# Three plain column pairs and a down projection ahead of the Strassen pairs, the last pair by token blocks, two weight roundings on ScalarE

## What is computed

```python
h = x * (1 + sc2) + sh2
u = h @ w_up + b_up                      # 1024 -> 5632
uc = conv_b + sum(conv_w[j] * ctx[:, j:j + T] for j in range(3))
a, g = jnp.split(uc, 2, axis=-1)
f = (a * jax.nn.gelu(g)) @ w_down        # 2816 -> 1024
x = layer_norm(ALPHA * x + g2 * f, ln2_w, ln2_b)
```

## Time and profile before

| | us |
|---|---|
| median of 3 runs (1894.36 to 1896.42) | 1895.5 |
| the profiled execution | 1895.79 |
| its span, first to last instruction | 1894.0 |
| TensorE busy in it | 1808.4 (95%) |
| GpSimd busy | 897.0 (47%) |
| VectorE busy | 1115.0 (59%) |
| ScalarE busy | 585.3 (31%) |

### The profile page before, as it was taken

One profiled execution on the slowest core, in us unless ns is written; L12 is line 12 of the kernel. 1 busy time (PEld: TensorE's weight loads), 2 busy tenths in 40 slices (PEclk: granted clock), 3 DMA queues, 4 the chain that ended last, 5 costly groups with the idle time before them and its releaser, 6 DMA issues.

```text
span 1894.0 us, 30856 instructions
## 1 busy us (share of the span) xinstructions
PE 1808.4 (95%) x12279; PEld 1733.2 (92%) x12279; DVE 1115.0 (59%) x2006; ACT 585.3 (31%) x1327; POOL 897.0 (47%) x638
## 2 busy tenths in 40 slices
PE   8999999999999999999999994999999999999884
PEld 6999888888999999899999994999999999999873
DVE  4837875773322324354345857875677567656677
ACT  3213444433222323342111675122122212211235
POOL 0332212212222222133336448688888888888830
PEclk9999999999999999999999996999999999999987
DMA  9443321114333434265333000111111111111102
GB/s 389 166 145 107 122 83 69 57 57 136 98 107 124 124 107 121 84 234 178 125 125 101 12 12 26 44 47 45 46 46 66 46 46 45 68 38 53 46 32 84
DMA packets 78903, 173.42 MB, mean 92 GB/s; under 512 B 9300, under 2 KB 42452, under 8 KB 78632
## 3 DMA queue, kind: packets, MB, share of 16 engines
q1 hardware_dynamic: 55112, 119.63, 18.6%
q10 hardware_dynamic: 23648, 51.82, 7.6%
HBM read 139.19 MB, written 32.24 MB: 91 GB/s over the span
## 4 chain that ended last, share of the span: by engine, by line
PE 84%; DVE 6%; ACT 3%; POOL 2%; DVEq 2%; DMA 1%; issue 1%; ACTq 0%; SPq 0%; POOLq 0%
PE acc L587 38%; PE px L868 12%; PE px L912 7%; PE acc L868 7%; PE acc L912 4%; PE px L834 2%; PE px L658 1%; PE acc L834 1%; PE px L687 1%; PE px L670 1%; PE px L684 1%; PE px L760 1%; PE px L759 1%; PE px L758 1%; PE px L672 1%
## 5 line engine op out<-in xcount | busy, mean ns | idle before, releaser
L587 PE MATMUL acc<-x_hilo_a,w_hilo 128*128 128x352 f32 x4032 | 664.3, 324 | 1.7 <-ACT x_c L1013 1.7
L587 PEld LDWEIGHTS acc<-x_hilo_a,w_hilo 128*128 128x128 f32 x4032 | 643.0, 188 | 9.9 <-issue 9.2
L458 POOL CAST w_hilo<-w_raw 128x1024 fp32r<-128x1024 f32 x71 | 81.3, 1146 | 731.7 <-PE acc L587 623.0
L460 POOL TENSOR_TENSOR w_hilo<-w_raw,w_hilo 128x1024 fp32r<-128x1024 f32 x71 | 184.9, 2604 | 5.7
L494 POOL TENSOR_TENSOR w_unit<-w_raw,w_unit 128x512 fp32r<-128x512 f32 x120 | 177.1, 1476 | 9.6
L868 PE MATMUL px<-x_hilo_a,w_unit 128*128 128x264 f32 x1200 | 157.1, 287 | 2.5 <-DVE x_hilo_a L1873 2.5
L868 PEld LDWEIGHTS px<-x_hilo_a,w_unit 128*128 128x128 f32 x1200 | 152.1, 191 | 2.7 <-DVE x_hilo_a L1873 2.7
L912 PE MATMUL px<-ffn_act,w_unit 128*128 128x352 f32 x900 | 152.5, 325 | 2.1 <-DVE u_row_g L1929 2.1
L912 PEld LDWEIGHTS px<-ffn_act,w_unit 128*128 128x128 f32 x900 | 146.2, 190 | 2.6 <-DVE u_row_g L1929 2.4
L492 POOL CAST w_unit<-w_raw 128x512 fp32r<-128x512 f32 x120 | 122.2, 1019 | 42.3 <-PE px L912 10.8
L1720 DVE SCALAR_TENSOR_TENSOR c_state<-c_state,stage,px 128x257 f32<-128x257 f32 x36 | 17.4, 482 | 207.1 <-PE px L760 207.1
(11 more groups left out here) (322 smaller groups left out, 2929.0 us busy)
## 6 DMA issues: line engine op xcount, KB each, us to landing
w_raw<-in_w_panels SPq DMA_DIRECT2D x141, 512.0 KB, 3.3
z_spill<-stage ACTq DMA_DIRECT2D x41, 528.0 KB, 2.7
adaT_ring<-in_w_adaT SPq DMA_DIRECT2D x32, 512.0 KB, 4.4
stage<-z_spill ACTq DMA_DIRECT2D x20, 528.0 KB, 4.7
ada_ring<-in_w_ada SPq DMA_DIRECT2D x16, 512.0 KB, 13.4
zc<-z_spill SPq DMA_DIRECT2D x8, 1024.0 KB, 9.3
...
```

What stands on the lines that cost most here:

```text
L458: nc.gpsimd.tensor_copy(to[:, 0, :], raw[:, s, :]).then_inc(w_hi, 1)
L460: nc.gpsimd.tensor_tensor(to[:, 1, :], raw[:, s, :], to[:, 0, :].bitcast(F32), ALU.subtract).then_inc(w_ready, 1)
L587: last = mm(acc[:, n, 0:NW], whl[:, slot, wi, k * P:(k + 1) * P], rhs[:, xi, k, n * NW:(n + 1) * NW], start=(k == 0 and j == 0), stop=(k = ...
```

## The change

1. **Three plain pairs.** `SINGLES` lists six plain panels: pair 2 is now plain, and the first Strassen pair is number 3 (`PAIR0`). Its terms stand in another order (A11, S2, A12, S3, S1, A22, S4).
2. **Down 0 ahead of pair 3.** The order is now: six plain panels, down 0, pairs 3 and 4, down 1, and the rest as before.
3. **Preparation moved.** The scaling of `XC` goes from DVE to POOL, four instructions ahead of each of the two added panel splits. ScalarE's and VectorE's lists at the start of the channel half are interleaved anew: the convolution of pair 0 stands between the block sums, `h_full` has two buffers of its own, and T1 is made out of `x_hilo_a` in place during down 0 (`t1_full`, `t1_high`, `t1_low`), since the sixth plain panel still reads the old values.
4. **Last pair by token blocks.** Taps, gelu, product and rounding of pair 21 run in three blocks of 352 (`last_block`, `last_gelu`, `last_round`), and the last down step waits for `fa_lo` block by block.
5. **Two of seven roundings on ScalarE.** The high parts of A12 and A22 are written by ScalarE (`plain_high`, after `first_take`); POOL waits for them and does the low part.

```diff
+SINGLES = ((0, 0), (0, 1), (1, 0), (1, 1), (2, 0), (2, 1))
+NSING = len(SINGLES)
+PAIR0 = 3
-    order = [("u", 0, i) for i in (0, 2, 1, 3)] + [("p", 1, 0), ("d", 0, 0), ("d", 0, 1)]
+    order = [("u", pi, r) for pi, r in SINGLES] + [("d", 0, 0), ("d", 0, 1)]
...
             def round_unit(unit, to, src):
                 count = UNIT_READY[unit]
-                nc.gpsimd.tensor_copy(to[:, 0, :], src).then_inc(w_hi, 1)
-                pool.wait_ge(w_hi, count)
+                if unit[1] in ("A12", "A22"):
+                    pool.wait_ge(a_hi, 2 * (2 * unit[0][1] + unit[0][2] - PAIR0) + (1 if unit[1] == "A12" else 2))
+                    pool.sem_inc(w_hi, 1)
+                else:
+                    nc.gpsimd.tensor_copy(to[:, 0, :], src).then_inc(w_hi, 1)
+                    pool.wait_ge(w_hi, count)
...
+            for kt in range(KH):
+                sums_low(kt)
+            for k in range(KT):
+                nc.gpsimd.tensor_scalar(XC[:, k, :], XC[:, k, :], der[:, 4, k:k + 1], der[:, 5, k:k + 1], ALU.mult, ALU.add)\
+                  .then_inc(xc_rdy, 1)
+                if k % 4 == 3:
+                    split(P_FFN + 4 + k // 4)
...
             def down_ready(j, m, n):
-                if n == 0 and m == 0:
-                    pe.wait_ge(fa_lo, j * 2 + 2)
+                if m == 0 and (n == 0 or j == FF - 1):
+                    pe.wait_ge(fa_lo, j * 2 + (n + 1 if j == FF - 1 else 2))
...
+            def plain_high(pi):
+                item = ("p", pi // 2, pi % 2)
+                for part, s in (("A12", 0), ("A22", 1)):
+                    p = PANEL[item] + s
+                    act.wait_ge(raw_in[p % 2], (p // 2 + 1) * 16)
+                    unit_free(act, (item, part))
+                    A(wu[:, UNIT_SLOT[item, part], 0, :], raw[:, p % 2, HALF:D], ACT.Copy).then_inc(a_hi, 1)
...
+            def t1_full(kt):
+                if kt == 0:
+                    dve.wait_ge(*ready(("u", *SINGLES[NSING - 1], NT - 1)))
+                V.tensor_tensor(u2t[:, :], XA[:, 0, kt, HN:T].bitcast(F32), XA[:, 0, kt, 0:HN].bitcast(F32), ALU.subtract)
+                dve.drain()
+                V.tensor_tensor(u2t[:, :], u2t[:, :], XA[:, 1, kt, HN:T].bitcast(F32), ALU.add)
+                dve.drain()
+                V.tensor_tensor(u2t[:, :], u2t[:, :], XA[:, 1, kt, 0:HN].bitcast(F32), ALU.subtract).then_inc(ts_rdy, 1)
...
+            dve.wait_ge(xc_rdy, KT)
+            down_row(0, 0)
+            t1_full(0)
+            down_row(0, 1)
+            t1_low(0)
+            conv_first(2, 1)
+            down_row(0, 2)
...
-            ffn_conv(2 * FF - 1, 1)
-            ffn_conv(2 * FF - 1, 0)
-            ffn_low(2 * FF - 2)
-            dve.drain()
-            ffn_prod(2 * FF - 1)
-            ffn_low(2 * FF - 1)
+            for n in range(NT):
+                last_block(n)
```

More of the change, by code:

```diff
@@ L264, in build @@
         lsum1 = at("ln_sums", [P, 2, T], o_T)
-        hb = at("h2_full", [P, 2, T], o_T)
-        t1f = after("h2_diff", [P, KH, HN])
+        hb = at("h2_full", [P, 2, 2, T], o_T)
+        assert place["end"] <= o_C
         wo = at("w_out_hilo", [P, KT - 2, 2, D], o_B, F32R)
@@ L272, in build @@
         cs = after("conv_out", [P, FG, 4, 4])
[L273 removed]
+        fc0 = after("ffn_consts_first", [P, 2, 4, 8])
         assert place["end"] <= 229344
@@ L1953, in down_row, with last_block @@
                     down_take(("d", j, m, n))
+            def last_block(n):
+                pi = 2 * FF - 1
+                a, b = n * NW, CW if n == NT - 1 else (n + 1) * NW
+                rows = [ST[:, conv_row(pi, r), a:b] for r in range(2)]
+                for tap in range(2):
+                    for r in (1, 0):
+                        dve.wait_ge(cv_a, row_made(pi, r))
+                        last = V.scalar_tensor_tensor(rows[r], ub[r][:, a + tap:b + tap], consts(pi, r)[:, 1 + tap:2 + tap], rows[r], ALU.mult, ALU.add)
+                        if tap:
+                            last.then_inc(cv_d, 1)
+                    dve.drain()
+                dve.wait_ge(gl_rdy, pi + n + 1)
+                V.tensor_tensor(rows[0], rows[0], rows[1], ALU.mult).then_inc(pr_rdy, 1)
+                for t in range(2):
+                    dve.wait_ge(fa_hi, pi + (n + 1 if t else 0))
+                    for c, d, s in pieces(n):
+                        last = V.tensor_tensor(ft[:, 1, t, c:d], ST[:, conv_row(pi - 1 + t, 0), c + 2 * s:d + 2 * s],
+                                               ft[:, 0, t, c:d].bitcast(F32), ALU.subtract)
+                last.then_inc(fa_lo, 1)
             sums_full(0)
@@ L1962, in _ @@
             t2_low(3)
[L1963 to L1964 removed]
             ffn_conv(1, 0)
[L1966 to L1967 removed]
             ffn_prod(0)
             ffn_conv(1, 1)
[L1970 removed]
             ffn_low(0)
             ffn_prod(1)
[L1973 to L1974 removed]
+            ffn_conv(2, 0)
             ffn_low(1)
[L1976 to L1982 removed]
+            dve.wait_ge(xc_rdy, KT)
[5 more added lines that the diff above has]
+            down_row(0, 2)
+            dve.drain()
+            conv_second(2, 1)
+            t1_full(1)
+            down_row(0, 3)
+            t1_low(1)
+            dve.drain()
+            t1_full(2)
+            down_row(0, 4)
+            t1_low(2)
+            dve.drain()
+            t1_full(3)
+            down_row(0, 5)
+            t1_low(3)
+            ffn_prod(2)
+            down_row(0, 6)
+            down_row(0, 7)
+            for pi in range(PAIR0, 2 * FF):
+                if pi == PAIR0:
+                    u2_take(pi)
+                    u3_take(pi)
+                    c22_take(pi)
+                    ffn_low(2)
+                    c21_take(pi)
+                    c12_take(pi)
+                elif pi % 2 and pi < 2 * FF - 2:
                     j, pv = pi // 2 - 1, pi - 1
```

271 lines of the change are left out of this document (137 added, 134 removed).

## The result

The changed kernel is **slower**: 1907.5 us (median of 4 runs, 1905.1 to 1909.6) against 1895.2 of the kernel before, a ratio of 1.0064 with a 95% interval of 1.0046 to 1.0081. I had forecast 1890.8 and a range up to 1902. The profiled execution took 1907.5 us with a span of 1905.6, 11.6 more than the span before.

What follows compares the result with a forecast made beforehand. TensorE, busy 95% of the span, was taken as the bound, with matmul count and few holes deciding. Start 0, roundings -2.3 and last pair -2.4 gave -4.7: 1890.8 us from 1895.5, forecast band 1886 to 1894, full range 1879.5 to 1902.

Steps and rivals of the forecast that it cites:

- hole: After the fourth plain panel: TensorE waits 26.0 us for POOL's scalings and split of the fifth, where it stood 22.0.
- wait at the start of down 0: Start of down 0: pair 1's product takes some 11.2 us against 11.5 of the sixth panel, a tie.
- down 0: Down 0: VectorE can't keep up, so 6.5 us are lost on top of TensorE's 23.0.
- tail: After pair 21: token blocks let VectorE start taking down tiles earlier, -2.4 us, bounded by -6.4 and +4.4.
- the first rival: Start of the channel half: POOL's scalings run at its two-input rate, together +11.3, giving 1902.1 us; chance 0.16.
- the 1.1 to 1.9 that I had named as a sign of being wrong: Before the fifth panel's split: the forecast would be wrong if one POOL scaling left 1.1 to 1.9 us.
- the -2.3 for the roundings: Pair 21: two casts moved to ScalarE bring POOL's low part 2.3 us earlier, shrinking the hole from 4.92 to 2.6.
- GpSimd would wait for ScalarE in every double pair: Double pairs: a new short hole in each, eight with slow clock costing over 15 us, would prove the forecast wrong.
- The cover that I named: Steady stretch: ScalarE's casts cost zero, since the low parts are due three terms (8.8 us) later.
- The rival that short instructions lose their turns: Last pair: VectorE's short block instructions wait for POOL's, last term +4.4, sum +2.1, 1897.6 us; chance 0.16.
- 34.6 us could be won: Plain work's end to pair 3: if nothing waited, pair 3 would begin at 1186.1, winning 34.6 us; not expected.
- VectorE keeps up: Faster rival in down 0: VectorE keeps up and scalings are cheap, the start gains 9 us, 1882; chance 0.20.

Runs made afterwards that it cites:

- e4: The changed kernel with pair 3's terms in the usual order (S1 third, A12 fifth): 1900.0 us.
- e2: The kernel before with only the high parts of A12 and A22 moved to ScalarE: 1896.3 us, ratio 1.0006.
- e5: The changed kernel with both added panel splits ahead of all eight scalings and pair 3's terms in the usual order: 1891.4 us.
- e6: e5 with all roundings on GpSimd again: 1889.6 us.
- e1: The kernel before with only the last pair by token blocks: 1895.3 us, ratio 0.9995.
- e11: e6 with the last pair whole again instead of by token blocks: 1889.8 us.
- e10: e9 with the roundings back on GpSimd and the first T1 block ahead of pair 1's product: 1887.8 us.
- e7: e5 without two of the three subtractions of each T1 block (output not the reference's): 1885.7 us.
- e9: e5 with panel splits between low-sum blocks, ScalarE's third-row takes before the last full rows, and first tap and gelu before the last high sums: 1888.8 us.
- e12: e10 with the eight scalings on ScalarE instead of GpSimd: 1887.8 us.

## Why the prediction was wrong

Its sum was -4.7, and the spans say +11.6. Step by step:

| step | predicted | measured |
|---|---|---|
| ScalarE's last high sums end | 1150.6 | 1150.7 |
| low sums end | 1154.1 | 1153.9 |
| four scalings | 7.5 | 9.0 |
| split of the fifth panel | 4.4 | 5.3 |
| hole | 26.0 | 29.5 |
| slow clock behind it | 2.4 | 2.2 |
| wait at the start of down 0 | about none (a tie) | none |
| down 0 | 29.5 | 31.2 |
| pair 3 begins | 1221.0 | 1224.5 |
| pair 3 to pair 5 | no change | +7.7 |
| pair 5 to the end of pair 21 | -2.3 | +3.2 |
| tail | -2.4 | -3.2 |

**The start was right in its mechanism and short in three terms.** The order of waits, their releasers and the first two times came as forecast. A scaling alone is 1.21 us (I had 1.15), so the first rival falls. The Trainium skill (GPSIMD Engine Reference, Engine selection) has one-input operations near line rate. The row agrees: 1.21 us where VectorE needs 1.32. What I took too small was the time beside VectorE: 0.7 us on each scaling was 1.04, and 0.6 on the split 1.55. At 2.25 us a scaling lies outside the 1.1 to 1.9 that I had named as a sign of being wrong. In down 0 the loss was 8.2 us instead of 6.5. The holes in it were shorter than forecast, 4.9 us instead of 5.7; the slow clock behind the last was a full one (24 matmuls in 6.94 us, granted clock 0.54 of full from 1217.7 to 1224.5), where I had counted less than half. Pair 3 begins 3.9 us later than before, and as this execution was 1.3 us ahead, the stretch is +5.1 instead of 0. By e4's trace, which has the same instructions there, it is +1.9 (90.4 us), so of the 5.1 up to 3.2 are the scatter of single executions.

**The step that failed is a term put at nothing without a reason: pair 3 to pair 5.** The changed order of pair 3's terms stood in my own description of the change, and in no term of the sum (0 - 2.3 - 2.4). It costs 7.5 us (e4), the largest single item of the miss. In the sum itself the step that failed is the -2.3 for the roundings, where that stretch came out at +3.2 and the roundings alone at +2.4 (e2) to +3.2 (e5 to e6). A slot of a ring is handed on in the order of the terms; moving S1 from third to fifth place holds its slot for two more terms, and the one who waits for it is S4's unit. I had named as a danger that GpSimd would wait for ScalarE in every double pair. It does, 47.7 us in all in e5, but no hole of TensorE came from it, only gaps of up to 0.5 us.

**The roundings had the wrong sign.** I took 2.3 us at pair 21 by shifting GpSimd's work, and zero elsewhere. e2 and e6 show +2.4 to +3.2 in the body and -0.9 to -1.1 in the tail. GpSimd got only 0.5 us of the 2.3 at pair 21 (39.2 us instead of 39.7), and the hole there is 4.1 to 4.5 us in the seven traces with the roundings on ScalarE and 4.4 to 4.9 in the six without. In the body the instructions that stay on GpSimd wait for ScalarE and then fall on VectorE's taps. The cover that I named (the low parts are due three terms later) held for TensorE's units, but not for VectorE. How VectorE's longer taps reach TensorE is argued: the gaps carry no releaser.

**The tail was right to 0.8 us by luck.** I gave the -2.4 to the blocks. Alone they bring 0.7 (e1) or 0.4 (e11 to e6), and the full gain is there only with the roundings on ScalarE too, where GpSimd is done at E + 10.3 to E + 12.1. The rival that short instructions lose their turns has something in it: in e6 GpSimd works until E + 12.3 and VectorE's first tile is at E + 18.8, and in e11, with pair 21 whole, it is at E + 18.1 though GpSimd works until E + 17.2. The exclusive lock of the Trainium skill (SBUF — State Buffer, Who interferes with whom) fits this and the 1.56 and 0.71 us of e10, though no run here shows the lock itself.

**And the ceiling.** I had reckoned that without holes 34.6 us could be won, and that "VectorE keeps up" would give 9. The runs show that down 0 belongs to VectorE (e7), and make it likely for the whole first stage: seven kernels with its work whole need 79.9 to 84.6 us from M to pair 3, against 88.5 before, so some 4 to 9 of the 34.6 us could be had by order. e7 gives 8 more than e5, by leaving out 8 of the 16 instructions of T1. VectorE is busy for 65.8 us of the stage in e5 and for 69.4 to 69.7 in e9, e10 and e12. Ahead of down 0 it also waits for ScalarE, 15.1 us in e5 and 5.3 in e9, so it is never fully loaded there; whether a shorter path over ScalarE gives more wasn't tried. Had I added up VectorE's work from M to the end of down 0, and not in down 0 alone, a floor of 66 to 70 us would have stood beside TensorE's 53.9, and at most 19 to 23 of the 34.6 us would have been left to win. Whether T1 can be made cheaper and right (the buffer for making it earlier lies where the first products are kept) wasn't tried.
